# One-hots of the first key: four tokens in one comparison on VectorE, the gates multiplied in by ScalarE

## The chip, the cores and the metric

The kernel runs on one core of a Trainium2 chip. The metric is the device time of one execution in microseconds, of which lower is better. Three executions of the kernel before took 4444.77, 4454.81 and 4462.94 us, the median being 4454.81.

TensorE multiplies matrices, VectorE and ScalarE work on elements, GpSimd issues gathers and scatters here, and SyncE issues the other DMAs. The engines run side by side and wait for each other by semaphores; each works through its own instructions in order.

## What is computed

The whole kernel is two blocks of a network over 512 tokens of width 1024: six feed-forward layers with two attention layers between them, a mixer layer, and at the end a PEER layer. Only the last one is touched. It finds for each token and each of 8 heads 16 experts out of 128 x 128, by two keys of 128 values each, and adds up the chosen experts with gates:

```python
i1 = jnp.take_along_axis(si[:, :, 0], ci // PEER_TOPK, axis=-1)
i2 = jnp.take_along_axis(si[:, :, 1], ci % PEER_TOPK, axis=-1)
eidx = i1 * PEER_N_KEYS + i2
g = jax.nn.softmax(cs, axis=-1)
u = expert_u[eidx]
v = expert_v[eidx]
act = jax.nn.gelu(jnp.einsum('td,thkd->thk', xb, u).astype(jnp.float32), approximate=False)
return jnp.einsum('thk,thkd->td', (g * act).astype(v.dtype), v)
```

## The kernel before, in words

For 384 of the 512 tokens the kernel doesn't gather the experts. It computes the products of all 16384 experts' u rows with the tokens, takes Gelu of them ("hidden", 64 units of two first keys each), multiplies them by a table of gates which is zero where an expert wasn't chosen, and multiplies that by all v rows. The remaining 128 tokens go another way, with rows gathered by GpSimd.

The table of gates has 128 x 128 x 384 entries in DRAM (`gates_added`). For 256 tokens GpSimd scatters the gates into it (L2881). For the other 128 tokens, the ones of this change, TensorE makes the table. For one token, `second` is a matrix of 128 slots (8 heads x 16) by 128 keys that has a 1 where the slot's second key is that key, and `first` is the same for the first key, with the slot's gate in place of the 1. Their product over the slots is the token's 128 x 128 piece of the table. `chosen` holds, with the slots on the partitions, the first keys (`chosen[:, 0]`), the second keys (`chosen[:, 1]`) and the gates (`chosen[:, 2]`) of the 128 tokens.

Four tokens are a quad, and there are 32 quads. VectorE builds a quad (`build`, L3020): one wide comparison L3026 makes `second` for four tokens, and four instructions L3030 make `first`, each for one token, comparing `iota` with the key and multiplying by the gate at once. `first` and `second` have a ring of three buffers (RING). TensorE multiplies (`spread_quads`, L3204, matmul L3210) into PSUM bank 6 or 7, and ScalarE copies the bank to `staged` (`stage`, L2809, copy L2814). When the 16 quads of a group are staged, SyncE stores 4 MB of them to `gates_added` (`store_gates`, L2707, DMA L2711). GpSimd's gathers L2889 begin when both stores have landed.

The quads are woven into 13 of the 64 hidden units (SPREAD_AT = 44 to 56; x is the number of the unit in this stretch, 0 to 12). `quads_of(x)` gives for each one quad "before" its first half and one or two "between" its halves, by turns one and two (`QUADS`, L2571). A hidden unit n is this: its tile of u arrives by four DMAs (L2678), which SyncE issues when `lo_ready` says that VectorE is done with the tile that used the buffer before (two buffers, so three units ahead of its use). VectorE transposes it in place (`turn`, L3009) once TensorE has finished unit n-2. ScalarE rounds it to w_hi (`turned_hi`, two casts L2787), and VectorE writes the remainder w_lo (`turned_lo`, two instructions L3016). TensorE makes the products in two halves of 24 matmuls (`hide_half`, L94 to L96). ScalarE takes the Gelu out of PSUM (`activate`, L2798), and SyncE stores the result (L2704).

The order is written out by hand on each engine, for x with n = 44 + x:
- VectorE: transpose n+1, build the "between" quads of x, w_lo of n+1, build the "before" quad of x+1.
- ScalarE: stage "before", cast w_hi of n+1, stage "between", Gelu of n.
- TensorE: spread "before", first half of n, spread "between", second half of n.

TensorE's wait in `spread_quads` is for `built` (VectorE's last instruction of the quad) and for `taken` (the staging of the quad two before, which frees the PSUM bank). VectorE's wait in `build` is for `spread` of the quad three before, which frees the ring. Behind the stretch come the last 7 hidden units, then 64 units of the v half (L3225 to L3227), which run beside the gathers, and then a final normalization and the output.

Of the kernel before, what the change touches and what calls it, by code (L numbers as in the profile page):

```python
# [19 lines left out]
ALU = mybir.AluOpType  # L20
# [2507 lines left out]
NH = 8  # L2528
# [39 lines left out]
QUAD = 4  # L2568
RING = 3
GROUP_QUADS = TG // QUAD  # L2570
QUADS = ((1, 1), (1, 2)) * 6 + ((1, 1),)  # L2571
# [10 lines left out]
def quads_of(x):  # L2582

    at = sum(sum(q) for q in QUADS[:x])
    a, b = QUADS[x]
    return range(at, at + a), range(at + a, at + a + b)
# [9 lines left out]
def peer(c, gain, w_q, sub_keys, u, v, h, hidden, h_rows):  # L2596

    nc = c.nc
# [4 lines left out]
    with ExitStack() as ph:  # L2603
        sb = lambda name, shape, dt=F32, on=ph: on.enter_context(nc.sbuf_tensor(f"pr_{name}", shape, dt))
        q = sb("q", [P, 2, 2, T])
        chosen = sb("chosen", [P, 3, P])
# [25 lines left out]
        with ExitStack() as spread_ph:  # L2632
            second = sb("second", [P, RING, QUAD, KEYS], on=spread_ph)
            first = sb("first", [P, RING, QUAD, KEYS], on=spread_ph)
# [16 lines left out]
                 "q_taken", "keys_turned", "keys_taken", "scored", "s_taken", "indexed", "steps",  # L2651
                 "shifted", "weighed", "rows_turned", "chosen_taken", "turned", "gelued", "built", "spread", "taken",
                 "written", "hi_done", "lo_done", "added", "placed", "scattered"))
        row_used, z_ready, acc_ready, gated = s_taken, weighed, shifted, indexed
        table = c.gates.rearrange("a p t -> (a p t)").unsqueeze(1)
        ps = c.psum
        keys_ps = ps[:, 4, 0:2 * P]
# [108 lines left out]
        def _(act):  # L2766
# [17 lines left out]
            def copy_hi(j):  # L2784

                for a in range(2):
                    ins = nc.scalar.copy(by_chunk(c.hi, j, a), turned_part(c, j, a))  # L2787
                ins.then_inc(c.hi_ready, 1)

            def turned_hi(n):  # L2790
                act.wait_ge(turned, n + 1)
                copy_hi(n % 2)

            def activate(n):
                act.wait_ge(c.tile_used, 2 * (uA + n // 2) + n % 2 + 3)
                act.wait_ge(stored[n % 2], 16 * (n // 2) + 16)
                at = 2 * (n % 2)
                nc.scalar.activation(q[:, n % 2, :, 0:W], ps[:, at:at + 2, 0:W], ACT.Gelu).then_inc(gelued, 1)  # L2798
# [6 lines left out]
            def take_chosen(r):  # L2805
                act.wait_ge(rows_turned, r + 2)
                nc.scalar.copy(chosen[:, r, :], ps[:, 6 + r % 2, 0:P]).then_inc(chosen_taken, 1)

            def stage(quads):  # L2809

                for k in quads:
                    g, at = k // GROUP_QUADS, k % GROUP_QUADS
                    act.wait_ge(spread, k + RING + 1)
                    nc.scalar.copy(staged[:, g, :, at * QUAD:(at + 1) * QUAD],  # L2814
                                   ps[:, 6 + k % 2, :].rearrange("p (t k) -> p k t", t=QUAD)).then_inc(taken, 1)
# [20 lines left out]
            for n in range(SPREAD_AT):  # L2836
# [4 lines left out]
                if n == CHOSEN_AT:  # L2841
                    take_chosen(0)
                    take_chosen(1)
            take_chosen(2)
            for x in range(len(QUADS)):
                n = SPREAD_AT + x
                before, between = quads_of(x)
                stage(before)
                turned_hi(n + 1)
                stage(between)  # L2850
                activate(n)
            for n in range(SPREAD_END, UNITS - 1):
                turned_hi(n + 1)
# [41 lines left out]
        def _(dve):  # L2895
            V = nc.vector
# [123 lines left out]
            def build(quads):  # L3020

                for k in quads:
                    dve.wait_ge(spread, k + 1)
                    wide = [P, QUAD, KEYS]
                    toks = slice(k * QUAD, (k + 1) * QUAD)
                    V.tensor_tensor(second[:, k % RING], c.iota[:, :].unsqueeze(1).broadcast_to(wide),  # L3026
                                    chosen[:, 1, toks].unsqueeze(2).broadcast_to(wide), ALU.is_equal)
                    for t in range(QUAD):
                        tok = k * QUAD + t
                        ins = V.tensor_scalar(first[:, k % RING, t, :], c.iota[:, :], chosen[:, 0, tok:tok + 1],  # L3030
                                              chosen[:, 2, tok:tok + 1], ALU.is_equal, ALU.mult)
                    ins.then_inc(built, 1)

            def weigh_hidden(m):
                j = m % 2
# [54 lines left out]
            turned_lo(SPREAD_AT)  # L3090
            dve.wait_ge(chosen_taken, 4)
            build(quads_of(0)[0])
            for x in range(len(QUADS)):
                n = SPREAD_AT + x + 1
                turn(n)
                build(quads_of(x)[1])
                turned_lo(n)
                if x + 1 < len(QUADS):
                    build(quads_of(x + 1)[0])
# [27 lines left out]
            for b in range(0, KD, 2):  # L3127
                x = c.x_t[:, b:b + 2, :]
# [3 lines left out]
        def _(pe):  # L3132
# [71 lines left out]
            def spread_quads(quads):  # L3204

                for k in quads:
                    pe.wait_ge(built, k + 1)
                    pe.wait_ge(taken, k + 1)
                    for t in range(QUAD):
                        mm = nc.tensor.matmul(ps[:, 6 + k % 2, t * KEYS:(t + 1) * KEYS], second[:, k % RING, t, :],  # L3210
                                              first[:, k % RING, t, :], start=True, stop=True)
                    mm.then_inc(spread, 1)
# [59 lines left out]
            for x in range(len(QUADS)):  # L3272
                before, between = quads_of(x)
                n = SPREAD_AT + x
                spread_quads(before)
                wait_tile(c, pe, uA + n // 2, n % 2)
                pe.wait_ge(gelued, n + 1)
                hide_half(n % 2, 0)
                spread_quads(between)
                hide_half(n % 2, 1).then_inc(c.tile_used, 1)  # L3280
# [124 lines left out]
def peer_layer(c, w):  # L3405

    nc = c.nc
    hidden = nc.dram_tensor("peer_hidden", [UNITS, P, 2, W], F32).ap()
    h_rows = nc.dram_tensor("peer_h_rows", [2, KD, P, T], F32).ap()
    w_q, keys, u, v = w["peer_w_q"][0], w["peer_sub_keys"][0], w["peer_u"][0], w["peer_v"][0]  # L3410

    def run(following):
        with ExitStack() as ph:
            h = splits(c, ph, "peer")
            peer(c, lambda k: vec_col(c, "ln_ffn", k), w_q, keys, u, v, h, hidden, h_rows)

    return Layer("peer", lambda use: wide_first(c, w_q, use), NH // 2 + UNITS, run)
# [90 lines left out]
```

## Time and profile before

| | |
|---|---|
| median of three runs | 4454.81 us |
| the profiled execution: time, span | 4455.52 us, 4453.8 us |
| TensorE busy in the span | 4104.0 us (92%) |
| VectorE | 2552.1 us (57%) |
| ScalarE | 1376.7 us (31%) |
| GpSimd | 934.2 us (21%) |
| HBM read, written | 562.38 MB, 65.14 MB |

The profile is of one execution. Times in it count from the start of the span. The stretch that the change touches lies at 3495 to 3640 us. A busy share over the whole span is a mean over stages with different limits, so the stretch is read by itself: windows give the busy time of each engine in it, groups gather instructions of one line, and timelines show the single instruction with its start, its duration and, in square brackets, the idle time of its engine ahead of it and what ended that. An instruction's duration overlaps the start of the next one on its engine by some 0.1 us, so what counts for a row of instructions is the distance between their starts. Spreading matmuls show two records for each matmul. PEclk is the granted clock of TensorE as a share of 2.4 GHz.

### The profile page before, as it was taken

To read this page: it belongs to the slowest core of one execution; us is meant where nothing else is said; L and a number is where in the kernel's file an instruction comes from. 1 tells how busy PE (TensorE), PEld (TensorE's weight loads), DVE (VectorE), ACT (ScalarE), POOL (GpSimd) and SP (SyncE) were. 2 spreads that over 40 slices of the span, in tenths; PEclk is the share of its full clock that TensorE was granted. 3 is DMA by queue.
4 is the path that set the end of the run, shared out by engine and by line. 5 is a ranking of instruction groups with operands and counts; after the bars stand their busy time and mean duration, and the time that the engine had idled before them with its cause. 6 is when DMAs were issued, how large, how long until landed. Compare 5 with 4: busy or idle time off the path is not lost. (4 is left out here: it accounts for less than half of the span.)

```text
span 4453.8 us, 56704 instructions
## 1 busy us (share of the span) xinstructions
PE 4104.0 (92%) x21307; PEld 3603.7 (81%) x21307; DVE 2552.1 (57%) x3600; ACT 1376.7 (31%) x1484; POOL 934.2 (21%) x628
## 2 busy tenths in 40 slices
PE   8999889999999999998999899988999998888787
PEld 7888667888888668887899688767999988888786
DVE  4333444334333664334777724347999867787776
ACT  3222443222222443223344312222333332222222
POOL 0000000000000000000111100003777764666661
PEclk9999999999999999998999999999999998899998
DMA  3235612223223122232111133325877799999994
GB/s 121 96 88 156 193 36 76 94 89 106 97 90 94 45 48 94 94 88 75 59 59 59 40 94 94 95 76 146 163 161 157 147 207 347 350 355 367 344 369 180
DMA packets 628339, 629.14 MB, mean 141 GB/s; under 512 B 115061, under 2 KB 565741, under 8 KB 628222
## 3 DMA queue, kind: packets, MB, share of 16 engines
q1 hardware_dynamic: 554494, 493.24, 36.5%
q0 software_dynamic: 73728, 134.38, 9.9%
q8 instruction: 68, 1.11, 0.1%
q14 instruction: 49, 0.40, 0.0%
HBM read 562.38 MB, written 65.14 MB: 141 GB/s over the span
## 5 line engine op out<-in xcount | busy, mean ns | idle before, releaser
L78 DVE TENSOR_TENSOR w_lo<-w_raw,w_hi 128x2048 fp32r<-128x2048 f32 (+2 forms) x326 | 667.1, 2047 | 584.7 <-ACT w_hi L72 584.4
L72 ACT CAST w_hi<-w_raw 128x2048 fp32r<-128x2048 f32 (+2 forms) x326 | 557.2, 1711 | 1141.9 <-PE psum L96 384.0
L94 PE MATMUL psum<-h_hi,w_hi 128*128 128x512 f32 x1552 | 612.1, 394 | 15.5 <-DVE w_lo L78 12.6
L96 PE MATMUL psum<-h_hi,w_lo 128*128 128x512 f32 x1552 | 607.0, 391 | 0.0
L95 PE MATMUL psum<-h_lo,w_hi 128*128 128x512 f32 x1552 | 606.8, 391 | 0.0
L2881 POOL DMA_INDIRECT gates_added<-pr_rows,pr_place x256 | 445.3, 1740 | 575.0 <-DVE pr_place L2950 444.3
L3225 PE MATMUL psum<-pr_act_hi,w_hi 128*128 128x384 f32 x1024 | 366.3, 358 | 109.6 <-DVE pr_act_lo L3043 109.4
L94 PE MATMUL psum<-h_hi_peer,w_hi 128*128 128x384 f32 (+1 forms) x1104 | 383.6, 347 | 50.4 <-DVE w_lo L3016 43.8
L95 PE MATMUL psum<-h_lo_peer,w_hi 128*128 128x384 f32 (+1 forms) x1104 | 377.4, 342 | 0.0
L96 PE MATMUL psum<-h_hi_peer,w_lo 128*128 128x384 f32 (+1 forms) x1104 | 377.0, 341 | 0.0
L3226 PE MATMUL psum<-pr_act_lo,w_hi 128*128 128x384 f32 x1024 | 361.3, 353 | 0.0
L94 PEld LDWEIGHTS psum<-h_hi,w_hi 128*128 128x128 f32 x1552 | 293.3, 189 | 82.5 <-issue 17.3
L3227 PE MATMUL psum<-pr_act_hi,w_lo 128*128 128x384 f32 x1024 | 359.7, 351 | 0.0
L95 PEld LDWEIGHTS psum<-h_lo,w_hi 128*128 128x128 f32 x1552 | 293.5, 189 | 61.5 <-issue 1.2
L96 PEld LDWEIGHTS psum<-h_hi,w_lo 128*128 128x128 f32 x1552 | 293.0, 189 | 61.8
L3225 PEld LDWEIGHTS psum<-pr_act_hi,w_hi 128*128 128x128 f32 x1024 | 207.4, 203 | 120.6 <-DVE pr_act_lo L3043 120.6
L94 PE MATMUL psum<-mix_h_hi,w_hi 128*128 128x264 f32 (+1 forms) x944 | 292.2, 310 | 5.7 <-ACT ssd_raw L1789 2.4
L95 PE MATMUL psum<-mix_h_lo,w_hi 128*128 128x264 f32 (+1 forms) x944 | 290.1, 307 | 0.0
L96 PE MATMUL psum<-mix_h_hi,w_lo 128*128 128x264 f32 (+1 forms) x944 | 290.0, 307 | 0.0
L719 PE MATMUL psum<-a_hi_ffn,w_hi 128*128 128x512 f32 x704 | 273.9, 389 | 0.0
L720 PE MATMUL psum<-a_lo_ffn,w_hi 128*128 128x512 f32 x704 | 273.9, 389 | 0.0
L721 PE MATMUL psum<-a_hi_ffn,w_lo 128*128 128x512 f32 x704 | 273.9, 389 | 0.0
(488 smaller groups left out, 7707.8 us busy)
## 6 DMA issues: line engine op xcount, KB each, us to landing
w_raw<-in_ffn_w_gate_up_dram SPq DMA_DIRECT2D x176, 512.0 KB
w_raw<-in_peer_u_dram SPq DMA_DIRECT2D x256, 256.0 KB
w_raw<-in_peer_v_dram SPq DMA_DIRECT2D x128, 512.0 KB
w_raw<-in_w_in_dram SPq DMA_DIRECT2D x64, 512.0 KB
w_raw<-in_ffn_w_down_dram SPq DMA_DIRECT2D x64, 384.0 KB
gates_added<-zeros SPq DMA_DIRECT2D x16, 1536.0 KB, 12.3
peer_hidden<-pr_q SPq DMA_DIRECT2D x64, 384.0 KB
pr_back<-peer_hidden SPq DMA_DIRECT2D x64, 384.0 KB
```

Source lines behind the costliest of these rows:

```text
L72: c.nc.scalar.copy(c.hi[:, slot, :cols], c.raw[:, slot, :cols]).then_inc(c.hi_ready, 1)
L78: c.nc.vector.tensor_tensor(c.lo[:, slot, :cols], c.raw[:, slot, :cols], c.hi[:, slot, :cols].bitcast(F32), ALU.subtract).then_inc(c.lo_re ...
L94: c.nc.tensor.matmul(out, w_hi, x_hi, start=(n == 0), stop=False)
L95: c.nc.tensor.matmul(out, w_hi, x_lo, start=False, stop=False)
L96: mm = c.nc.tensor.matmul(out, w_lo, x_hi, start=False, stop=(n == last))
L719: nc.tensor.matmul(ps[:, 4 + bank, :], w_hi[:, k, :], a_hi[:, f, :], start=first, stop=False)
L720: nc.tensor.matmul(ps[:, 4 + bank, :], w_hi[:, k, :], a_lo[:, f, :], start=False, stop=False)
L721: mm = nc.tensor.matmul(ps[:, 4 + bank, :], w_lo[:, k, :], a_hi[:, f, :], start=False, stop=final)
L2881: pool.indirect_dma_start(out=table, out_offset=bass.IndirectOffsetOnAxis(ap=place[:, t, k:k + 1], axis=0), in_=rows[:, 2, t, k:k + 1], in ...
L3225: nc.tensor.matmul(ps[:, d, 0:W], w_hi[:, a, col], act_hi[:, j, a, 0:W], start=start, stop=False)
L3226: nc.tensor.matmul(ps[:, d, 0:W], w_hi[:, a, col], act_lo[:, j, a, 0:W], start=False, stop=False)
L3227: mm = nc.tensor.matmul(ps[:, d, 0:W], w_lo[:, a, col], act_hi[:, j, a, 0:W], start=False, stop=stop)
```

## The change

VectorE makes `first` of a quad with one wide comparison, like `second`, without the gates. ScalarE then multiplies each token's 128 columns in place by the token's gate (a scale for each partition), four instructions for a quad, and signals `sized`, which is the semaphore `keys_turned` used again (it stands at NH + 2 = 10 by then). TensorE waits for `sized` in place of `built`. ScalarE's new function `scale` is called for the first quad ahead of the stretch, for the "between" quads right behind the cast of w_hi and ahead of their staging, and for the next "before" quad ahead of the Gelu.

```diff
-        row_used, z_ready, acc_ready, gated = s_taken, weighed, shifted, indexed
+        row_used, z_ready, acc_ready, gated, sized = s_taken, weighed, shifted, indexed, keys_turned
...
+            def scale(quads):
+
+                for k in quads:
+                    act.wait_ge(built, k + 1)
+                    for t in range(QUAD):
+                        tok = k * QUAD + t
+                        one = first[:, k % RING, t, :]
+                        ins = nc.scalar.mul(one, one, chosen[:, 2, tok:tok + 1])
+                    ins.then_inc(sized, 1)
...
             take_chosen(2)
+            scale(quads_of(0)[0])
             for x in range(len(QUADS)):
                 n = SPREAD_AT + x
                 before, between = quads_of(x)
                 stage(before)
                 turned_hi(n + 1)
+                scale(between)
                 stage(between)
+                if x + 1 < len(QUADS):
+                    scale(quads_of(x + 1)[0])
                 activate(n)
...
-                    for t in range(QUAD):
-                        tok = k * QUAD + t
-                        ins = V.tensor_scalar(first[:, k % RING, t, :], c.iota[:, :], chosen[:, 0, tok:tok + 1],
-                                              chosen[:, 2, tok:tok + 1], ALU.is_equal, ALU.mult)
-                    ins.then_inc(built, 1)
+                    V.tensor_tensor(first[:, k % RING], c.iota[:, :].unsqueeze(1).broadcast_to(wide),
+                                    chosen[:, 0, toks].unsqueeze(2).broadcast_to(wide), ALU.is_equal).then_inc(built, 1)
...
-                    pe.wait_ge(built, k + 1)
+                    pe.wait_ge(sized, NH + 2 + k + 1)
```

## Rows read from the trace of the kernel before

**Rows 1.** Windows by stage: us, busy and instructions by engine, PEclk, DMA share, GB/s.

```profile
3495.00:3640.00 145.00, 139.14 (x868) 138.12 (x869) 112.83 (x199) 54.77 (x72) 109.38 (x63) 0.98 0.81 158
...
3640.00:3800.00 160.00, 129.71 (x680) 127.42 (x679) 105.46 (x122) 39.58 (x36) 77.99 (x52) 0.89 1.00 328
```

**Rows 2.** Groups, 3490 to 3645: busy us, mean ns, idle before.

```profile
L3030 DVE TENSOR_SCALAR pr_first<-iota,pr_chosen 128x128 f32<-128x128 f32 x128 | 36.9, 386 | 0.0
...
L3026 DVE TENSOR_TENSOR pr_second<-iota,pr_chosen 128x512 f32<-128x512 f32 x32 | 21.4, 668 | 3.0 <-ACT pr_chosen L2807 3.0
```

**Rows 3.** Timeline of VectorE, one unit: start us, us, line op.

```profile
3530.51 2.31 DVE L3009 STREAM_TRANSPOSE w_raw<-w_raw 128x2048 f32<-128x2048 f32 x1 [1.63 <-PE psum L96]
3532.74 0.65 DVE L3026 TENSOR_TENSOR pr_second<-iota,pr_chosen 128x512 f32<-128x512 f32 x1
3533.31 1.14 DVE L3030 TENSOR_SCALAR pr_first<-iota,pr_chosen 128x128 f32<-128x128 f32 x4
3534.37 0.67 DVE L3026 TENSOR_TENSOR pr_second<-iota,pr_chosen 128x512 f32<-128x512 f32 x1
...
3535.99 2.35 DVE L3016 TENSOR_TENSOR w_lo<-w_raw,w_hi 128x1024 fp32r<-128x1024 f32 x2
...
3538.86 1.11 DVE L3030 TENSOR_SCALAR pr_first<-iota,pr_chosen 128x128 f32<-128x128 f32 x4
```

**Rows 4.** Timeline of ScalarE, the cast of the same unit.

```profile
3532.85 2.00 ACT L2787 CAST w_hi<-w_raw 128x1024 fp32r<-128x1024 f32 x2 [0.94 <-issue]
```

**Rows 5.** Timeline of TensorE, the spreading matmuls of four quads or pairs.

```profile
3508.91 1.05 PE L3210 MATMUL psum<-pr_first,pr_second 128*128 128x128 f32 x8
...
3513.97 2.15 PE L3210 MATMUL psum<-pr_first,pr_second 128*128 128x128 f32 x16
...
3520.13 1.05 PE L3210 MATMUL psum<-pr_first,pr_second 128*128 128x128 f32 x8
...
3530.24 1.05 PE L3210 MATMUL psum<-pr_first,pr_second 128*128 128x128 f32 x8
```

**Rows 6.** Timelines of VectorE and TensorE at the first quad.

```profile
3495.30 0.69 DVE L3026 TENSOR_TENSOR pr_second<-iota,pr_chosen 128x512 f32<-128x512 f32 x1 [2.99 <-ACT pr_chosen L2807]
...
3497.12 1.50 PE L3210 MATMUL psum<-pr_first,pr_second 128*128 128x128 f32 x8 [2.74 <-issue]
```

**Rows 7.** ScalarE instructions with one operand from SBUF; then two back to back.

```profile
L446 ACT ACTIVATE h_hi<-x_t,vec 128x512 fp32r<-128x512 f32 x48 | 34.5, 718 | 66.8 <-DVE x_t L643 66.8
...
L1357 ACT ACTIVATE sw_sink<-sw_top,rows 128x4 f32<-128x4 f32 x16 | 4.5, 282 | 0.0
...
1680.85 0.71 ACT L446 ACTIVATE h_hi<-x_t,vec 128x512 fp32r<-128x512 f32 x1
1681.47 0.62 ACT L448 ACTIVATE square<-x_t 128x512 f32<-128x512 f32 x1
```

**Rows 8.** Timelines of VectorE, ScalarE and TensorE at the late tile.

```profile
3598.99 2.31 DVE L3009 STREAM_TRANSPOSE w_raw<-w_raw 128x2048 f32<-128x2048 f32 x1 [6.30 <-DMA w_raw<-in_peer_u_dram]
...
3601.34 1.99 ACT L2787 CAST w_hi<-w_raw 128x1024 fp32r<-128x1024 f32 x2 [5.60 <-DVE w_raw L3009]
...
3602.96 3.71 PE L3210 MATMUL psum<-pr_first,pr_second 128*128 128x128 f32 x16 [3.67 <-DVE pr_first L3030]
```

**Rows 9.** Timeline of SyncE's DMA queue, the two gate stores.

```profile
3574.65 0.56 SPq L2711 DMA_DIRECT2D gates_added<-pr_staged  x1
...
3643.84 0.56 SPq L2711 DMA_DIRECT2D gates_added<-pr_staged  x1
```

**Rows 10.** Timeline of VectorE, the late tile behind the second store.

```profile
3668.41 2.31 DVE L3009 STREAM_TRANSPOSE w_raw<-w_raw 128x2048 f32<-128x2048 f32 x1 [10.97 <-DMA w_raw<-in_peer_u_dram]
```

**Rows 11.** ScalarE groups, table loads before Exp in this layer.

```profile
L2782 ACT ACT_TABLE_LOAD x7 | 9.0, 1283 | 0.1
```

**Rows 12.** Windows, granted clock as PEclk, at the first quad and in another stage.

```profile
3495.00:3500.00 5.00, 2.88 (x13) 2.91 (x14) 4.70 (x9) 1.58 (x4) 2.88 (x2) 0.77 1.10 236
...
2125.00:2150.00 25.00, 19.95 (x155) 18.80 (x155) 17.55 (x33) 9.95 (x17) 2.40 (x4) 1.00 0.18 58
```

## The prediction

> **What bounds the kernel now.** I read the windows by stage first, then the groups of the stretch that the change touches, and last the timelines of single instructions, with the waits that stand in them. The edit acts only in 13 hidden units of the PEER layer, from 3495 to 3640 us. In that window TensorE is busy 139.14 of 145 us, VectorE 112.83 and ScalarE 54.77 [rows 1]. So TensorE sets the pace there, and the reader is to see that the engine that the change relieves (VectorE) has 32 us to spare already. The idle time of TensorE before the spreading matmuls L3210 is two waits, 2.74 us at the start and 3.67 us where a tile is late [rows 6, 8]. The removed L3030 is 36.9 us of VectorE and the kept L3026 21.4 us [rows 2].
>
> The timelines show one steady unit, the one whose "before" quad TensorE starts at 3530.24. I call such a start T0 [rows 5]. VectorE starts to transpose the next tile at T0+0.27, when the old unit's products are out, then builds two quads, writes w_lo from T0+5.75 and builds the next "before" quad until T0+9.7 [rows 3]. ScalarE casts w_hi from T0+2.61 to T0+4.61 and has only the staging of the "between" quads to do behind it [rows 4]. TensorE reaches the "between" quad 5.06 us after its T0 (3508.91 to 3513.97) and has no gap there, because VectorE has the first "between" quad at T0+4.2 (3533.31 and 1.14 us) [rows 3, 5]. That T0+5.06 is the due time of everything the change adds.
>
> **VectorE's part.** Four L3030 and one L3026 make a quad of 1.63 us (3532.74 to 3534.37) [rows 3]. After the change a quad is two wide comparisons of the L3026 kind. Those are 0.67 us by the mean [rows 2], but the instruction behind one starts 0.57 us after it (3532.74 to 3533.31), so with 0.03 to spare a quad is 1.2 us. That saves 0.43 us a quad, 14 us over 32 quads. All of it lies beside TensorE's work: w_lo can start 0.8 us earlier in units with two "between" quads, but TensorE wants it only at the next unit, more than 11 us after T0, and it was there at T0+8.1 [rows 3]. I cost the saving at nothing. Its cover is TensorE's 139 of 145 us [rows 1]; without it, the 14 us would be the most there is. Load requests of SyncE that hang on w_lo go out up to 0.8 us earlier, which only matters where a tile is late, below.
>
> **ScalarE's part.** It gets 128 multiplications of 128x128 with a scale read from SBUF. No such instruction runs before, so I bound it. The two nearest forms have one such operand: 128x4 takes 282 ns, 128x512 takes 718 ns [rows 7]. The line between them gives 388 ns at 128 columns. Back to back, the instruction behind the 0.71 us one starts 0.62 us later, an overlap of 0.09 us [rows 7]. So four take 3 x 0.30 + 0.39 = 1.28 us. The lower bound is 4 x 0.19 = 0.76 us (0.28, the 128x4 form, less the overlap); the upper one is 4 x 0.39 = 1.56 us with no overlap. I take 1.28, since both rows are of the same kind.
>
> **What lands on the path.** TensorE now waits for ScalarE's last multiplication instead of VectorE's last comparison. ScalarE is held by its cast until T0+4.61, though VectorE's new quad is there at T0+3.8. The multiplications start under the cast's tail at about T0+4.52 and end at T0+5.80; with about 0.05 us for the signal TensorE may start at T0+5.85 instead of T0+5.06. That is 0.79 us, and 0.1 us more because the first weight load is no longer hidden under running matmuls: 0.89 us for each steady unit. In a unit with two "between" quads the second is ready 4 x 0.30 = 1.2 us after the first, and TensorE comes for it after 0.96 + 0.1 us (3513.97 has 16 records over 2.15 us, two quads) [rows 5], 0.14 us more.
>
> The other waits that the change adds are covered. The next "before" quad of a two-quad unit is built at T0+9.7 less 0.8 (the earlier w_lo) less 0.4 (its own wide comparison), and scaled by T0+9.8; TensorE wants it at T0+11.2 and 0.9 later (the period is 3508.91 to 3520.13, and 10.1 for a unit with one [rows 5]). Behind it on ScalarE stands the Gelu of the unit TensorE is still on, which cannot start earlier anyway, and behind the "between" multiplications stand only the copies of PSUM to `staged`, which wait for TensorE's spreading. No DMA is issued from ScalarE. What ScalarE delays next is `taken`, and with it the two 4 MB gate stores of SyncE.
>
> **The sum**, unit by unit (x = 0 to 12).
> - x = 0: the first build starts at 3495.30 and TensorE at 3497.12 [rows 6]. New: 1.25 us of comparisons, 0.05, 1.28 of multiplications, 0.05 give 3497.93, so +0.8. Its "between" quad comes 6.7 us later, at a slow clock, and is in time.
> - x = 1 to 6: 6 x 0.89 = 5.3, and 3 x 0.14 = 0.4 for the three with two quads.
> - x = 7 and 8: nothing. The first gate store leaves at 3574.65 [rows 9], and the tile for x = 9 then comes 6.30 us late at 3598.99 [rows 8]. The landing moves with the store; 1.8 us more of TensorE's work before it only shortens that idle time.
> - x = 9: TensorE started at 3602.96, just behind VectorE's build. ScalarE's cast starts at 3601.34 and takes 1.99 [rows 8]; with 1.28 - 0.09 + 0.05 behind it TensorE starts at 3604.57, so +1.6.
> - x = 10 to 12: 3 x 0.89 + 0.14 = 2.8.
>
> Together 0.8 + 5.7 + 1.6 + 2.8 = **10.9 us**. With the bounds of the multiplication the steady wait is 0.37 or 1.17 us and the sum 5 or 14 us. Behind the window the second gate store leaves at 3643.84, after the last staging [rows 9], and all that follows hangs on it or on later units: the tile loads that wait behind it (10.97 us of VectorE idle before 3668.41 [rows 10]), the gathers of GpSimd, the v half. So I pass the shift on in full. The profiled execution took 4455.52 us (span 4453.8 and 1.7 around it), 0.7 above the median 4454.81. 4455.5 + 10.9 = 4466.4, or 4465.7 on the median: **4466 us**.
>
> **Rivals.**
> - *The long transfers give some of it back.* After 3640 the DMA engines are at full share (1.00 from 3640 to 3800 [rows 1]), and idle time of 10.97 us for a late tile stands there. If those landings depend less on the window's end than I think, part of the shift vanishes as in x = 7 and 8. For: the same thing happens behind the first store. Against: the store that causes it is itself moved. Half given back is +5: 4460.
> - *Not slower.* The same mechanism in full: the landing before 3668.41 is not moved at all, and its 10.97 us of idle time swallow the 10.9. It decides from the point where the idle time exceeds the shift. Result: 4455, or 1 us under it by the earlier load requests. Against it is that the first tile load behind the store waits for TensorE's units as well.
> - *A table load.* If the multiplication needs another function table than Gelu, ScalarE loads one of 1.283 us [rows 11] before each group of multiplications and again before Gelu. Only the first is on the path: 1.28 more in 11 places, +14, in all +25: 4480. For: Exp and Gelu switch like that in this layer, 7 times [rows 11]. Against: the copies and casts stand between Gelus with no load, and the scaled copy is the same function.
> - *The clock.* If a gap of 0.9 us in each unit brings TensorE from 2.4 to 1.2 GHz, a unit of 10.1 us nearly doubles, +8 us x 13 = +100. The clock does fall over the 2.74 us gap, to 0.77 in that stretch [rows 12]. Against: in the stretch at 2125, TensorE stands idle 5 of 25 us at a granted clock of 1.00 [rows 12].
>
> On the table rival the Trainium skill, "ScalarE: Activation LUTs", section "Table sets: the hidden batching unit", says that cheap functions such as copy stand in every set, so that they force no load. The trace agrees for copies and casts between two Gelus; no run here yet shows the multiplication. By that rule the sum stays 4466 instead of 4480. The same page's "Rules for kernel authors" sends multiplications to VectorE and so speaks against this change; by it the move costs time, as in the sum.
>
> **How the numbers follow.** Forecast (+6 to +15) 0.62; half given back 0.15; not slower 0.09; table load 0.05; clock 0.03; the rest, 0.06, is what other timing of transfers in the last 800 us does in either direction (the three runs shown lie from 4444.77 to 4462.94). The range takes in the cost bounds 4460 to 4470, the giving back down to 4455, the table case, and some 5 us of the scatter: 4450 to 4481. A difference under 0.5%, 22 us, is about what a measurement of this kernel can tell from no change. Faster by more needs a gain that no row offers: 0.03. Slower by more is the clock, half of the table case and an upper cost with scatter: 0.10. Within: 0.87.
>
> **What the profile after would show.** Right: a wait of about 0.8 us of L3210 for ScalarE in 10 to 12 units, "before" quads without a wait, unit periods of 11.0 and 12.3 instead of 10.1 and 11.2 us, multiplications of about 0.39 us that start 0.3 us apart and begin right behind the cast, VectorE's stretch 14 us less busy, ScalarE's about 40 us more, the clock at 1.00 between 3505 and 3590. Wrong: table loads at the new line, a first wait longer than 1.2 us, or a window that ends 11 us later while the end of the kernel does not.

## The result, and the profile after

The changed kernel takes 4460.57 us by the median of 20 executions (4442.37 to 4468.52), the kernel before 4451.25 us on the same occasions (4426.79 to 4462.94). The ratio of the changed kernel to the one before is 1.0024, with a 95% interval of 1.0013 to 1.0034, that is +10.7 us (+6 to +15); the two medians lie 9.3 us apart. Forecast were +10.9 us, and 4466 us for the time itself, which started from 4455.5 us for the kernel before where 20 executions now give 4451.25.

The page's line of busy time shows the trade. VectorE has 13.5 us less than before, ScalarE 38.6 us more, and TensorE the same work.

```profile
PE 4105.0 (92%) x21307; PEld 3598.4 (81%) x21307; DVE 2538.6 (57%) x3504; ACT 1415.3 (32%) x1612; POOL 935.1 (21%) x628
```

The groups by line and form of the changed kernel, 3480 to 3660 us (busy us, mean ns, idle before and what ended it); they answer to [rows 2]. L3042 is the new wide comparison, L2816 is the multiplication and L3221 the spreading matmul.

```profile
L2816 ACT ACTIVATE pr_first<-pr_first,pr_chosen 128x128 f32<-128x128 f32 x128 | 40.2, 390 | 4.5 <-DVE pr_first L3042 4.5
L3221 PE MATMUL psum<-pr_first,pr_second 128*128 128x128 f32 x256 | 38.1, 296 | 13.8 <-ACT pr_first L2816 10.2 <-issue 3.6
...
L3042 DVE TENSOR_TENSOR pr_first<-iota,pr_chosen 128x512 f32<-128x512 f32 x32 | 21.9, 683 | 0.0
```

The 36.9 us of L3030 have become 21.9 us of L3042, and ScalarE has 40.2 us of multiplications of 390 ns. TensorE's matmul now waits 10.2 us for ScalarE in the whole stretch, where it waited 3.67 us for VectorE before, at the late tile alone [rows 8].

TensorE's timeline (start us, us, records; in brackets its idle time and what ended it), which answers to [rows 5]:

```profile
3524.78 1.05 PE L3221 MATMUL psum<-pr_first,pr_second 128*128 128x128 f32 x8
...
3530.62 1.16 PE L3221 MATMUL psum<-pr_first,pr_second 128*128 128x128 f32 x8 [0.63 <-ACT pr_first L2816]
...
3535.79 1.05 PE L3221 MATMUL psum<-pr_first,pr_second 128*128 128x128 f32 x8
...
3541.64 2.33 PE L3221 MATMUL psum<-pr_first,pr_second 128*128 128x128 f32 x16 [0.63 <-ACT pr_first L2816]
...
3547.97 1.05 PE L3221 MATMUL psum<-pr_first,pr_second 128*128 128x128 f32 x8
```

A unit with one quad between its halves starts at 3524.78 and ends at 3535.79, 11.01 us where it was 10.11; one with two takes 12.18 us (to 3547.97) where it was 11.2. The quad between the halves starts 5.84 us into the unit where it started at 5.06. The bracket says 0.63 us only: the idle time counts from the end of the matmul ahead, which the profile models. The distance of the starts shows the whole 0.8.

The unit of 3535.79 on ScalarE and then on VectorE; the rows answer to [rows 4] and [rows 3]:

```profile
3538.41 2.00 ACT L2787 CAST w_hi<-w_raw 128x1024 fp32r<-128x1024 f32 x2 [0.94 <-DVE w_raw L3023]
3540.31 2.45 ACT L2816 ACTIVATE pr_first<-pr_first,pr_chosen 128x128 f32<-128x128 f32 x8
```

```profile
3538.30 0.65 DVE L3040 TENSOR_TENSOR pr_second<-iota,pr_chosen 128x512 f32<-128x512 f32 x1
3538.86 0.68 DVE L3042 TENSOR_TENSOR pr_first<-iota,pr_chosen 128x512 f32<-128x512 f32 x1
3539.46 0.69 DVE L3040 TENSOR_TENSOR pr_second<-iota,pr_chosen 128x512 f32<-128x512 f32 x1
...
3540.67 2.36 DVE L3030 TENSOR_TENSOR w_lo<-w_raw,w_hi 128x1024 fp32r<-128x1024 f32 x2
```

VectorE has the first quad ready at 3539.54 (3538.86 and 0.68), in the middle of ScalarE's cast. ScalarE turns to it at 3540.31, as the cast runs out, and needs 1.28 us for four tokens (2.45 for the eight of the two quads). TensorE starts at 3541.64.

The late tile behind the first gate store, which answers to [rows 8] and [rows 9] (SyncE, VectorE, ScalarE, TensorE):

```profile
3583.94 0.56 SPq L2711 DMA_DIRECT2D gates_added<-pr_staged  x1
...
3608.32 2.31 DVE L3023 STREAM_TRANSPOSE w_raw<-w_raw 128x2048 f32<-128x2048 f32 x1 [5.71 <-DMA w_raw<-in_peer_u_dram]
...
3610.66 1.99 ACT L2787 CAST w_hi<-w_raw 128x1024 fp32r<-128x1024 f32 x2 [3.58 <-DVE w_raw L3023]
3612.56 2.44 ACT L2816 ACTIVATE pr_first<-pr_first,pr_chosen 128x128 f32<-128x128 f32 x8
...
3613.89 3.78 PE L3221 MATMUL psum<-pr_first,pr_second 128*128 128x128 f32 x16 [3.26 <-ACT pr_first L2816]
```

From the store to the landing it is 24.38 us, before it was 24.34; from the landing to TensorE's start 5.57 us, before 3.97.

For whole traces I compare the stretch, from the start of VectorE's first build to the start of the Gelu of the last of the 13 units (unit 56), and the rest, from there to the end of the span. Starts and lengths are in us and from one trace each; the ratio (95% interval) is that of the timed executions where several were taken, and leaves out three far above all others (4946.53 and 11931.85 us of the kernel before, 5847.85 us of VectorE's part alone).

| kernel | first build | Gelu of unit 56 | stretch | rest | ratio to before |
|---|---|---|---|---|---|
| before | 3495.30 | 3642.31 | 147.0 | 811.5 | |
| before, again | 3496.03 | 3643.12 | 147.1 | 801.2 | |
| changed | 3498.26 | 3657.28 | 159.0 | 799.3 | 1.0024 (1.0013 to 1.0034) |
| changed, again | 3496.76 | 3656.08 | 159.3 | 811.0 | 1.0027 (1.0013 to 1.0041) |
| VectorE's part alone | 3496.65 | 3643.00 | 146.4 | 808.0 | 0.9981 (0.9961 to 1.0000) |
| the same, again | 3496.61 | 3642.76 | 146.2 | 801.2 | 0.9990 (0.9975 to 1.0006) |
| ScalarE's part alone | 3497.56 | 3660.33 | 162.8 | 805.9 | 1.0024 (1.0012 to 1.0036) |
| one multiplication | 3495.68 | 3642.42 | 146.7 | 804.2 | 0.9994 (0.9979 to 1.0010) |
| two multiplications | 3499.71 | 3650.46 | 150.8 | 797.4 | |
| eight | 3497.02 | 3693.24 | 196.2 | 805.6 | 1.0070 (1.0049 to 1.0091) |
| eight, again | 3495.01 | 3694.31 | 199.3 | 802.7 | |
| changed, one unit ahead | 3496.20 | 3643.75 | 147.6 | 796.2 | 1.0001 (0.9986 to 1.0016) |
| before, one unit ahead | 3494.75 | 3641.74 | 147.0 | 819.5 | 0.9996 (0.9981 to 1.0011) |

### The profile page after: what moved, and what is told of

Read it like the earlier page. It is cut to its first block and busy times, and to the rows that moved or that the text cites. A ratio compares the mean times of both kernels' runs of the same rounds, so it can differ in the third digit from the quotient of the medians.

```text
span 4456.6 us, 56736 instructions
## 1 busy us (share of the span) xinstructions
PE 4105.0 (92%) x21307; PEld 3598.4 (81%) x21307; DVE 2538.6 (57%) x3504; ACT 1415.3 (32%) x1612; POOL 935.1 (21%) x628
## 5 line engine op out<-in xcount | busy, mean ns | idle before, releaser
L2895 POOL DMA_INDIRECT gates_added<-pr_rows,pr_place x256 | 444.6, 1737 | 573.6 <-DVE pr_place L2964 444.3
```

Source lines behind the costliest of these rows:

```text
L2895: pool.indirect_dma_start(out=table, out_offset=bass.IndirectOffsetOnAxis(ap=place[:, t, k:k + 1], axis=0), in_=rows[:, 2, t, k:k + 1], in ...
```

## Experiments

The theory is that TensorE, which has no slack in the stretch, comes for the quad between the halves before ScalarE is done with it, and that the cost is the distance between the two moments. The rivals are that VectorE's new form or its effect on transfers costs, the handing over itself costs, ScalarE's 40 us cost wherever they stand, or that the rest of the kernel gives time back. Each edit is shown against the changed kernel, but for VectorE's part alone, where it is against the kernel before.

**ScalarE's part alone.** VectorE compares and multiplies as before, and ScalarE multiplies by ones.

```diff
-                        ins = nc.scalar.mul(one, one, chosen[:, 2, tok:tok + 1])
+                        ins = nc.scalar.mul(one, one, c.ones[:, 0:1])
...
-                    V.tensor_tensor(first[:, k % RING], c.iota[:, :].unsqueeze(1).broadcast_to(wide),
-                                    chosen[:, 0, toks].unsqueeze(2).broadcast_to(wide), ALU.is_equal).then_inc(built, 1)
+                    for t in range(QUAD):
+                        tok = k * QUAD + t
+                        ins = V.tensor_scalar(first[:, k % RING, t, :], c.iota[:, :], chosen[:, 0, tok:tok + 1],
+                                              chosen[:, 2, tok:tok + 1], ALU.is_equal, ALU.mult)
+                    ins.then_inc(built, 1)
```

> VectorE's work is that of before (four instructions that compare and multiply by the gate), and ScalarE still multiplies the four tokens in place, by a column of ones, so that the result is the same and only ScalarE's part of the change is left. Theory A (the time comes from TensorE waiting for ScalarE at the quad between the halves): all of the cost stays, steady waits of 0.6 to 0.7 us of L3210 for ScalarE in the same units, unit periods of 11.0 and 12.3 us, and 1.0022 to 1.0030 of before (+10 to +13 us), 1 us more than the change at most because VectorE's quads come 0.4 us later. Rival B (the time comes from VectorE's new form, or from what its earlier w_lo does to the transfers): within 3 us of before.

Its ratio is 1.0024, the whole cost. TensorE's timeline (L3224 is the spreading matmul here):

```profile
3537.11 1.05 PE L3224 MATMUL psum<-pr_first,pr_second 128*128 128x128 f32 x8
...
3542.96 1.16 PE L3224 MATMUL psum<-pr_first,pr_second 128*128 128x128 f32 x8 [0.62 <-ACT pr_first L2816]
...
3544.29 1.16 PE L3224 MATMUL psum<-pr_first,pr_second 128*128 128x128 f32 x8 [0.17 <-ACT pr_first L2816]
...
3549.45 1.05 PE L3224 MATMUL psum<-pr_first,pr_second 128*128 128x128 f32 x8
```

The wait of 0.62 us is there, 5.85 us into the unit, and this period is 12.34 us. The second of two quads waits 0.17 us more, since VectorE's quads come later. The stretch is 162.8 us, 3.8 over the change's, of which I expected 1. The steady units account for 0.7 us of it. At the first quad TensorE starts 3.13 us behind the first build instead of 2.71, and its first half then takes 8.00 us instead of 6.56; the units of the late tile, where TensorE stood 4.35 us instead of 3.26, take 1.2 us more.

**VectorE's part alone.** The wide comparison, TensorE waiting for VectorE, and nobody multiplying.

```diff
-                    for t in range(QUAD):
-                        tok = k * QUAD + t
-                        ins = V.tensor_scalar(first[:, k % RING, t, :], c.iota[:, :], chosen[:, 0, tok:tok + 1],
-                                              chosen[:, 2, tok:tok + 1], ALU.is_equal, ALU.mult)
-                    ins.then_inc(built, 1)
+                    V.tensor_tensor(first[:, k % RING], c.iota[:, :].unsqueeze(1).broadcast_to(wide),
+                                    chosen[:, 0, toks].unsqueeze(2).broadcast_to(wide), ALU.is_equal).then_inc(built, 1)
```

> VectorE makes the one-hots of the first key with the wide comparison, TensorE waits for VectorE as before, and nobody multiplies by the gates: that multiplication is left out, so the output is not the reference's. Only VectorE's part of the change is left. Theory A: TensorE reaches the quad between the halves 5.05 us after the unit's start with no wait, periods 10.1 and 11.2 us as before, VectorE some 14 us less busy in the stretch, and the time within 2 us of before (0.9995 to 1.0002, the first quad 0.5 us and the late tile 0.4 us earlier). Rival B: +8 us or more, 1.0018 and above.

The stretch is 0.7 us shorter than before, near the 0.9 expected, but in other parts. The first quad is 0.4 us earlier and one-quad units are those of before. Two-quad units take 11.00 us instead of 11.2, 0.7 us in all, because the second quad is ready when TensorE comes (two quads take 1.95 us instead of 2.15 to 2.17). The units around the late tile take 0.5 us more. TensorE's timeline (L3207):

```profile
3520.82 1.05 PE L3207 MATMUL psum<-pr_first,pr_second 128*128 128x128 f32 x8
...
3525.88 1.05 PE L3207 MATMUL psum<-pr_first,pr_second 128*128 128x128 f32 x8
...
3530.93 1.05 PE L3207 MATMUL psum<-pr_first,pr_second 128*128 128x128 f32 x8
```

The time, 0.9981 of before, lay under what this explains, so I ran it again.

> The same as the run with VectorE's part alone, taken again, since its time (0.9981 of before, 0.9961 to 1.0000) lay under what its stretch showed (0.7 us shorter than before). The multiplication by the gates is left out, so the output is not the reference's. If the stretch is all there is, 0.9995 to 1.0000 and an interval that holds it; if the lighter VectorE gives something elsewhere, 0.998 again with an interval below 1.

0.9990 with an interval that holds 1, and a stretch of 146.2. By the ratios the two lie 8.5 and 4.5 us under before where the stretch gives 0.7 to 0.9. Neither interval excludes no difference; a gain of some us outside the stretch is neither shown nor ruled out. What is shown is that VectorE's form costs nothing.

**One and two multiplications per quad**, the rest of the gates left out (the edit shown is for one; for two it is `range(2)`).

```diff
-                    for t in range(QUAD):
+                    for t in range(1):
                         tok = k * QUAD + t
                         one = first[:, k % RING, t, :]
```

> The changed kernel with one multiplication per quad on ScalarE instead of four: the gates of three of four tokens are left out, so the output is not the reference's. Theory A (the cost is the distance by which ScalarE's multiplications end behind the moment at which TensorE comes): the one ends some 0.4 us behind the cast, 0.05 to 0.1 us before TensorE's due time 5.05 us into the unit, so the steady waits vanish, periods are 10.1 and 11.2 us, the stretch is within 1.5 us of before (the late tile still 0.7 us later) and the time 0.999 to 1.001 of before. Rival (each handing over from VectorE to ScalarE to TensorE costs by itself, however short the work): waits of 0.3 us or more stay in each unit, and the stretch is 4 us or more longer than before.

> The changed kernel with two multiplications per quad on ScalarE: the gates of two of four tokens are left out, so the output is not the reference's. If the wait is a plain distance, the two end 0.59 us earlier than the change's four, and TensorE's unit periods of 11.02 and 12.18 us shrink by 0.59 to 10.4 and by about as much, with the weight load out of cover, to 11.5; the steady wait of the trace, 0.63 us with four, all but vanishes or is under 0.1. The stretch is 4 to 6 us longer than before.

TensorE's timelines (L3221), first with one, then with two:

```profile
3520.31 1.05 PE L3221 MATMUL psum<-pr_first,pr_second 128*128 128x128 f32 x8
...
3525.36 1.07 PE L3221 MATMUL psum<-pr_first,pr_second 128*128 128x128 f32 x8
...
3530.43 1.05 PE L3221 MATMUL psum<-pr_first,pr_second 128*128 128x128 f32 x8
```

```profile
3524.98 1.05 PE L3221 MATMUL psum<-pr_first,pr_second 128*128 128x128 f32 x8
...
3530.24 1.16 PE L3221 MATMUL psum<-pr_first,pr_second 128*128 128x128 f32 x8
...
3535.41 1.05 PE L3221 MATMUL psum<-pr_first,pr_second 128*128 128x128 f32 x8
```

With one, the period is 10.12 us and the steady waits are gone, though the hand-over from VectorE over ScalarE to TensorE is still there: beyond 0.01 to 0.02 us a unit, the handing over costs nothing by itself. With two, the quad between the halves starts 5.26 us into the unit and the period is 10.43 us, as expected; its stretch is 3.7 us over before, a little under the 4 to 6. With four it is 5.84 and 11.01. Two multiplications more are 0.58 us more: from a point between one and two on, the cost is a plain distance.

**Eight per quad.** The second key's one-hots are multiplied by ones ahead of the first key's.

```diff
                     for t in range(QUAD):
+                        two = second[:, k % RING, t, :]
+                        nc.scalar.mul(two, two, c.ones[:, 0:1])
+                    for t in range(QUAD):
```

> The changed kernel with twice as many multiplications on ScalarE: ahead of the four of a quad it multiplies the four tokens of the second key's one-hots by a column of ones, in place, which changes no value. Eight take 2.45 us instead of 1.28. Theory A with the wait as a plain distance: the steady wait of TensorE grows by 1.18 us to some 1.8, in units with two quads it waits once more by 1.3 us, periods 12.2 and 14.8 us; the stretch is some 29 us longer than before, 17 over the change, and if the rest of the kernel passes it on, 1.006 to 1.007 of before. If the rest gives part back: a stretch longer by the same 29 us but 1.005 or less. Rival (clock): pauses of 1.8 us bring the granted clock under 1.00 in the stretch, and the units are longer by several us more, 1.01 and above.

> The kernel with eight multiplications per quad, unchanged. In its first trace the stretch was 49 us longer than before, 20 over the distance sum of 29, with a granted clock of 0.66 to 0.86 in many of its 10 us windows. If that is the answer of the clock to pauses of 1.8 and 1.2 us, a second trace shows windows under 1.00 spread over the stretch again, with a stretch from 29 (the clock holds) to 50 us longer, and the total follows the stretch from run to run.

The waits are near those expected, 1.79 and at most 1.18 us, but many units are longer than the 12.2 and 14.8 us forecast for one and for two quads (up to 13.8 and 17.0 us). TensorE's timeline of one (L3224), and windows of 20 us (busy and instructions by engine, granted clock as PEclk, DMA share, GB/s):

```profile
3570.20 1.05 PE L3224 MATMUL psum<-pr_first,pr_second 128*128 128x128 f32 x8
...
3577.22 1.47 PE L3224 MATMUL psum<-pr_first,pr_second 128*128 128x128 f32 x8 [1.80 <-ACT pr_first L2819]
3579.55 2.07 PE L3224 MATMUL psum<-pr_first,pr_second 128*128 128x128 f32 x8 [0.87 <-ACT pr_first L2819]
...
3587.13 1.05 PE L3224 MATMUL psum<-pr_first,pr_second 128*128 128x128 f32 x8
```

```profile
3540.00:3560.00 20.00, 17.02 (x107) 16.51 (x106) 9.89 (x10) 14.40 (x38) 16.95 (x11) 0.99 0.65 103
3560.00:3580.00 20.00, 15.54 (x93) 14.61 (x92) 13.50 (x16) 15.83 (x40) 10.75 (x6) 0.95 0.56 105
3580.00:3600.00 20.00, 18.21 (x91) 17.89 (x91) 7.05 (x7) 11.61 (x30) 16.46 (x10) 0.80 0.64 109
```

This unit took 16.93 us, and the clock behind its two waits is partly at the lower level (0.80 in the third window). So here both are right: the distance for some 29 us, and the clock rival for most of the other 20 to 23. The traced stretches are 49 and 52 us longer than before, and the totals of these two executions 4500.84 and 4498.85 us follow them. Of the five other executions timed with the first, four lay lower, at 4471 to 4487 us, and the median gives 1.0070, +31 us, near the distance sum of 29. The mean granted clock of whole executions goes the same way: 0.958 in the three at 4499 to 4501 us, 0.960 and 0.961 at 4486, 0.962 at 4477 and 0.963 at 4471. So the lower level was shorter in the faster ones; in which part of the kernel can't be told without traces of them, and the kernel before shows the same order (0.961 at 4452 to 4460, 0.968 at 4424).

**One unit ahead, in both kernels.** The quads of unit x+1 are built behind w_lo of unit x, and with the change scaled ahead of the Gelu. The kernel before gets the lines with `build` alone.

```diff
             scale(quads_of(0)[0])
+            scale(quads_of(0)[1])
...
-                scale(between)
                 stage(between)
                 if x + 1 < len(QUADS):
                     scale(quads_of(x + 1)[0])
+                    scale(quads_of(x + 1)[1])
                 activate(n)
...
             build(quads_of(0)[0])
+            build(quads_of(0)[1])
...
                 turn(n)
-                build(quads_of(x)[1])
                 turned_lo(n)
                 if x + 1 < len(QUADS):
                     build(quads_of(x + 1)[0])
+                    build(quads_of(x + 1)[1])
```

> The changed kernel with the quads between the halves built and scaled one unit earlier: VectorE builds all quads of unit x+1 behind w_lo of unit x, and ScalarE scales them all ahead of the Gelu. The work of both engines is that of the change. Theory A: no wait for ScalarE at these quads, periods back to 10.1 and 11.2 us, only the first quad waits (3.6 us as in the change), and at the late tile TensorE no longer stops between the halves but at the start of the next unit. The time is that of before or up to 5 us less: 0.9988 to 1.0003. Rival B (ScalarE's added 40 us or the transfers cost by themselves wherever they stand): 1.0015 and above. Rival C: the Gelu, now up to 1.7 us later, makes TensorE wait at unit starts, with such waits in the trace.

> The kernel before, with all quads of unit x+1 built behind w_lo of unit x, the instructions unchanged (VectorE compares and multiplies, ScalarE doesn't). It is what is left of the shift in time alone, without ScalarE. The steady units have no wait before and none after. At the late tile TensorE is no longer stopped at the quad between the halves but at the next unit's first quad, which VectorE builds behind the late w_lo: a start some 1.3 us behind that w_lo, where the earlier experiment with ScalarE in it took 2.4. The stretch should be 1 to 4 us shorter than before, and the time 0.9988 to 1.0002 of before; if it is longer than before, building ahead costs TensorE at unit starts.

The changed kernel, one unit ahead, is the proof by removal: the same work on the same engines costs nothing that can be measured once it ends before TensorE comes. TensorE's timeline (L3223), steady units and the one behind the late tile:

```profile
3521.63 1.05 PE L3223 MATMUL psum<-pr_first,pr_second 128*128 128x128 f32 x8
...
3531.74 1.05 PE L3223 MATMUL psum<-pr_first,pr_second 128*128 128x128 f32 x8
...
3542.74 1.05 PE L3223 MATMUL psum<-pr_first,pr_second 128*128 128x128 f32 x8
...
3610.63 1.44 PE L3223 MATMUL psum<-pr_first,pr_second 128*128 128x128 f32 x8 [4.41 <-ACT pr_first L2816]
```

The periods are 10.11 and 11.0 us, the stretch is 147.6 us and the ratio 1.0001 (within 7 us either way). But the gain that I expected at the late tile is missing in both. The quads of the unit behind it are now built after the late w_lo. VectorE's w_lo and first build in the kernel before, one unit ahead, and TensorE's (L3211) start of that unit:

```profile
3603.50 2.42 DVE L3016 TENSOR_TENSOR w_lo<-w_raw,w_hi 128x1024 fp32r<-128x1024 f32 x2 [2.06 <-ACT w_hi L2787]
3605.84 0.68 DVE L3026 TENSOR_TENSOR pr_second<-iota,pr_chosen 128x512 f32<-128x512 f32 x1
3606.44 1.10 DVE L3030 TENSOR_SCALAR pr_first<-iota,pr_chosen 128x128 f32<-128x128 f32 x4
...
3607.60 2.08 PE L3211 MATMUL psum<-pr_first,pr_second 128*128 128x128 f32 x8 [3.38 <-DVE pr_first L3030]
...
3615.38 1.05 PE L3211 MATMUL psum<-pr_first,pr_second 128*128 128x128 f32 x8
```

Its unit starts 14.55 us after the last one (3593.05, the same trace) where it was 16.82 before, so 2.3 us were won. Then the clock is at the lower level (1.2 GHz, a PEclk of 0.50), and the first half takes 7.78 us (to 3615.38) instead of 5.05: 2.7 lost. In the kernel before, that slow stretch stood behind the quad between the halves. The idle time was moved, not taken away, and its slow restart went with it. So neither version beats the kernel before by anything that these runs can tell.

**Both kernels again.**

> The kernel before, unchanged, for a second trace. It tells how much the part behind the stretch (811.5 us from the Gelu of unit 56 to the end in the first trace) varies by itself. If it varies by 5 us or more, no difference of that part between single traces of two kernels can be read as theirs; the stretch itself should be within 1 us of 147.0.

> The changed kernel unchanged, for a second trace and a time on the same chip as the others. Theory A: the stretch is again 158 to 160 us (12 us over before), 1.001 to 1.004 of before. If the part behind the stretch, 799 us in the first trace, is 795 to 812 us, it lies where that of the kernel before lies (811.5 and 801.2), and no give-back can be read from it.

The stretches repeat to 0.3 us. The rest of the kernel is 811.5 and 801.2 us before and 799.3 and 811.0 changed, and over all traces in the table 796 to 820, with no relation to the kernel. It is this part that makes single traces of one kernel differ by 10 us. Most of that lies late in it. From the Gelu of unit 56 to that of unit 63, the last one, it is 77.0 to 80.2 us in all traces, and from there to the end 716.7 to 740.1 us.

One piece of the rest does go with the kernel: the late tile behind the second gate store, which answers to [rows 9] and [rows 10]. SyncE's store and VectorE's transpose in the changed kernel:

```profile
3658.81 0.56 SPq L2711 DMA_DIRECT2D gates_added<-pr_staged  x1
...
3681.94 2.31 DVE L3023 STREAM_TRANSPOSE w_raw<-w_raw 128x2048 f32<-128x2048 f32 x1 [9.53 <-DMA w_raw<-in_peer_u_dram]
```

From the store to the landing it is 23.13 us, in the changed kernel's second trace 23.17, where it was 24.57 and 24.47 before. From the Gelu of unit 56 to that of unit 59 it is 28.90 and 28.94 us where it was 30.34 and 30.24. So 1.4 us are given back there in both traces. Up to the Gelu of unit 63 it is 78.5 and 77.1 us instead of 79.9 and 79.8, that is 1.4 to 2.8. The four other traces whose steady units wait for ScalarE (two multiplications, ScalarE's part alone, eight twice) also have a way of 29.1 us or less from unit 56 to 59, and those without such a wait 29.7 or more. Why the landing comes sooner no run shows. GpSimd's last scatter L2881 (L2895 in the changed kernel) starts at 3645.17 before, beside the store, and at 3645.90 in the changed kernel, 13 us ahead of it, which may be the reason.

## Why the prediction was right

**The bound.** The step that TensorE sets the pace in the stretch and VectorE has room held: VectorE's 13.5 us, taken alone, shorten the stretch by 0.7 to 0.9 us where the prediction put nothing, and ScalarE's part alone has the whole cost (1.0024).

**Prices.** The multiplication was put at 388 ns and four at 1.28 us, from two forms of other sizes with one operand from SBUF [rows 7]; they measured 390 ns (mean) and 1.28 us. The quad of wide comparisons was put at 1.2 us and takes 1.16 to 1.21.

**The steady units.** Put at 0.89 us and 0.14 more with two quads. Measured 0.90 and, with two, 0.93 to 0.98 in all, so the 0.14 was 0.03 to 0.08. From the start of x = 1 to that of x = 7 (3508.91 to 3572.93 before, 3512.58 to 3582.22 changed) the sum was 5.7 and is 5.6. The cover of all other waits held: no "before" quad of a steady unit waits.

**The first quad.** Put at 0.8; from the first build to TensorE it is 2.71 us instead of 1.82, so 0.9, and the rest of x = 0 is 0.2 shorter.

**x = 7 to 9.** Put at 1.6. The quads of x = 7 and 8 did wait, but the landing moved with the store and absorbed it, and between landing and start came 1.60 us more, both as written; but the three units together lost 2.7 us. The missing 1.0 is the way from TensorE's restart to the next unit, 8.96 us instead of 7.92. Windows of 2 us around the restart (busy and instructions by engine, PEclk, DMA share, GB/s), before from 3602 and changed from 3613:

```profile
3602.00:3604.00 2.00, 1.04 (x7) 1.04 (x8) 2.00 (x8) 1.33 (x2) 1.70 (x2) 0.89 1.15 251
3604.00:3606.00 2.00, 1.93 (x9) 1.64 (x9) 2.00 (x5) 0.59 (x1) 1.70 (x2) 0.50 0.78 77
3606.00:3608.00 2.00, 2.00 (x12) 2.00 (x11) 2.00 (x5) 0.59 (x1) 1.70 (x2) 0.76 0.34 11
```

```profile
3613.00:3615.00 2.00, 1.11 (x5) 1.11 (x6) 2.00 (x3) 2.00 (x7) 0.00 (x0) 0.56 0.39 73
3615.00:3617.00 2.00, 2.00 (x11) 2.00 (x11) 1.48 (x3) 0.59 (x2) 1.75 (x1) 0.50 0.25 50
3617.00:3619.00 2.00, 2.00 (x9) 2.00 (x8) 0.00 (x0) 1.30 (x4) 1.70 (x2) 0.50 0.98 209
3619.00:3621.00 2.00, 2.00 (x10) 2.00 (x10) 0.00 (x0) 0.47 (x2) 1.70 (x2) 0.74 1.15 235
```

Before, the clock is back within 3606 to 3608, some 4 us after the restart at 3602.96; in the changed kernel within 3619 to 3621, some 6 us after 3613.89. By the PEclk of these windows the lower level (0.50) lasts 3.4 us in all before and 6.8 in the changed kernel. The term mis-sized is this restart, which I took as unchanged. It repeats, with 8.73 us in the changed kernel's second trace against 7.85 in that of before. But it isn't the doing of ScalarE's lateness, or not of that alone: VectorE's part alone, which has none, needs 8.59 and 8.69 us for the same way, after pauses of 3.53 and 3.25 us.

**x = 10 to 12.** Put at 2.8, measured 3.0.

**The rest does not pass the shift on in full.** The stretch grew by 12.0 and 12.2 us, and 1.4 us of that went at the second late tile, up to 2.8 by unit 63. The rival that gives back a part was right in kind, if not in size: half of 12 us is +6, at the lower end of the interval of the total (6 to 15). What the last 720 us and more do with the shift can't be read from traces that differ by 10 us there.

**What was luck.** The mechanism and the price of each wait came out as written. That the sum of 10.9 us meets the measured 10.7 within 0.2 is luck, with an interval of 6 to 15: the restart at the late tile was put 1.0 us too low, and some 1.4 us or more that came back behind the stretch were put at nothing. These two all but cancel. The time itself was forecast 5.4 us too high (4466 against 4460.57), 4.3 us of it from the 4455.5 us that the forecast started from. And 0.5% (22 us) was too wide as what can be told apart: 20 executions of each kernel told 0.24%.

**The rivals.** "Not slower" fell with the interval. The table load did not come: in the changed kernel's groups L2816 stands as ACTIVATE alone and the cast, the 128 multiplications, the staging and the Gelu run from 3480 to 3660 us without a load between them. The Trainium skill ("ScalarE: Activation LUTs", section "Table sets: the hidden batching unit") says that cheap functions such as copy stand in every table set. The trace agrees for the multiplication with a scale too. The clock stayed at 1.00 in the steady units with their pauses of 0.8 us:

```profile
3505.00:3590.00 85.00, 80.58 (x503) 77.58 (x501) 56.82 (x61) 53.49 (x116) 65.19 (x38) 1.00 0.70 134
```

It can't be dismissed, though: with eight multiplications it takes part in the cost.

**The forecast of signs.** The trace before could tell this much because the due time of every quad, 5.06 us into the unit, and ScalarE's cast, free at 4.6, could both be read; some 0.45 us were left for work of 1.28.

## What to carry to other kernels

When work is handed to an idle engine, its busy share (here 38%) says nothing: read when that engine is free in the period, when the bounding engine comes, and whether the work fits between. Where it doesn't fit, move it a period ahead, which here brought 40 us of ScalarE's work to no measurable cost. And where the engine relieved was not the bound, there is little to win: here the stretch was 0.7 to 0.9 us shorter by VectorE's part alone.

## What the runs showed of the hardware

Two things I had not expected. With eight multiplications TensorE paused 1.8 us in each unit and once more, 0.9 to 1.2 us, in every second one, and its granted clock was 0.76 to 0.99 in windows of 20 us; with pauses of 0.8 us in units of 11 to 12 us it stayed at 1.00.

The other is the restart behind the late tile. For the way of one half unit and two quads the traces show (us of idle time, then us of way):

| kernel | idle | way |
|---|---|---|
| before | 3.67 | 7.92 |
| before, again | 3.83 | 7.85 |
| one multiplication | 4.09 | 7.67 |
| two multiplications | 3.61 | 8.49 |
| VectorE's part alone | 3.53 | 8.59 |
| the same, again | 3.25 | 8.69 |
| changed | 3.26 | 8.96 |
| changed, again | 3.75 | 8.73 |
| ScalarE's part alone | 4.35 | 8.91 |

In the first three the clock was at the lower level for 3.4 us and in the other six for 6.8. Where a kernel has two traces they agree within 0.3 us. The length of the pause doesn't order them (8.91 after the longest, 7.67 after the next), and no run tells what does. So a restart is worth some 1 us in a forecast, either way, when an edit moves it.
